# Latent attention rebuilt: three rounded passes for scores and output product, one pipeline over 40 tiles

## The reference

```python
def blocked_attention(q_nope, q_rope, k_nope, k_rope, v):
    scale = 1.0 / math.sqrt(MLA_NOPE + MLA_ROPE)
...
        s = jnp.einsum('bqhd,bkhd->bhqk', qn, k_nope) + jnp.einsum('bqhd,bkd->bhqk', qr, k_rope)
        p = jax.nn.softmax(s.astype(jnp.float32) * scale, axis=-1).astype(v.dtype)
        return jnp.einsum('bhqk,bkhe->bqhe', p, v)
...
def mla_latent(h, ckv_ctx, krope_ctx, cos, sin, w_in, q_norm, kv_norm, w_q_b, w_kv_b, w_out):
...
    k_nope = jnp.concatenate([k_nope_c, k_nope_l], axis=1)
    k_rope_all = jnp.concatenate([krope_ctx, k_rope], axis=1)
    o = blocked_attention(q_nope, q_rope, k_nope, k_rope_all, v)
    return o.reshape(b, n, MLA_HEADS * MLA_V) @ w_out
```

## Time and profile before

| what | us |
|---|---|
| median of 3 runs | 2439.28 (2438.9 to 2439.61) |
| profiled execution | 2436.64 |
| its span | 2434.8 |
| retention, router, mixture of layer 0 (to) | 1352 |
| latent attention: front (from 1352 to) | 1485.76 |
| heads (to) | 1691.89 |
| output product (to) | 1763.26 |
| router and mixture of layer 1 (to) | 2434.8 |

### The profile page before, as it was taken

How to read it: one execution, slowest core, us unless ns; L and a number is a source line. 1 busy time by engine, 2 the same in 40 slices (tenths; PEclk the granted TensorE clock), 3 DMA queues, 4 the chain that set the end, 5 groups by cost and what they waited for, 6 DMA issues and landing times.

```text
span 2434.8 us, 26516 instructions
## 1 busy us (share of the span) xinstructions
PE 2268.7 (93%) x9712; PEld 1502.3 (62%) x9712; DVE 1715.2 (70%) x1882; ACT 1256.0 (52%) x1314; POOL 192.7 (8%) x227
## 2 busy tenths in 40 slices
PE   6999999999986999999999888988959999999995
PEld 2867868768654666666666454554436666666663
DVE  2675665757757899998998441332368998999996
ACT  3321312213135877778776333332347778777773
POOL 1000000000031011001000200000020001110001
PEclk9999999999998999999999899999979999999998
DMA  7443434525355999999998110100069999999991
GB/s 264 126 134 105 138 121 148 163 98 162 102 201 191 360 349 344 360 364 349 354 339 307 45 72 1 36 1 0 1 233 343 357 361 354 357 346 345 339 361 61
DMA packets 167649, 529.10 MB, mean 217 GB/s; under 512 B 13525, under 2 KB 22282, under 8 KB 167306
## 3 DMA queue, kind: packets, MB, share of 16 engines
q1 hardware_dynamic: 162954, 515.35, 59.1%
q0 software_dynamic: 2304, 8.39, 1.0%
q10 hardware_dynamic: 2304, 4.20, 0.5%
HBM read 516.72 MB, written 11.17 MB: 217 GB/s over the span
## 4 chain that ended last, share of the span: by engine, by line
PE 90%; DVE 4%; ACT 3%; issue 1%; POOL 1%; DMA 0%; SPq 0%; POOLq 0%; ACTq 0%; DVEq 0%
PE ps L1606 86%; PE ps L1609 4%; POOL SMALL L578 0%; POOL SMALL L577 0%; ACT W L308 0%; ACT W_HI L308 0%; DVE IDX L1363 0%; DVE B L1189 0%; DVE X L1190 0%; DMA REGION<-in_ada_b_dram 0%; DVE MIXREG L1362 0%; DVE REGION L1581 0%; DVE B L1164 0%; DVE ROUTE L1365 0%; ACT B L722 0%
## 5 line engine op out<-in xcount | busy, mean ns | idle before, releaser
L1401 DVE TENSOR_TENSOR W_LO<-RAW_W,W_HI 128x2048 fp32r<-128x2048 f32 x384 | 867.8, 2287 | 80.2 <-ACT W_HI L308 76.6
L308 ACT ACTIVATE W_HI<-RAW_W 128x2048 fp32r<-128x2048 f32 x384 | 726.4, 1917 | 197.8 <-PE ps L1606 196.8
L1606 PE MATMUL ps<-W_HI,XET_HI 128*80 128x512 f32 x1024 | 323.6, 397 | 17.4 <-issue 11.4
L1606 PE MATMUL ps<-W_LO,XET_HI 128*80 128x512 f32 x1024 | 320.9, 395 | 0.0
L1606 PE MATMUL ps<-W_HI,XET_LO 128*80 128x512 f32 x1024 | 320.8, 395 | 0.0
L1606 PEld LDWEIGHTS ps<-W_HI,XET_HI 128*80 128x80 f32 x1024 | 151.7, 149 | 98.4 <-issue 13.6
L1606 PEld LDWEIGHTS ps<-W_LO,XET_HI 128*80 128x80 f32 x1024 | 152.5, 149 | 86.3 <-issue 1.9
L1606 PEld LDWEIGHTS ps<-W_HI,XET_LO 128*80 128x80 f32 x1024 | 152.5, 149 | 85.2 <-issue 2.1
L1133 DVE SCALAR_TENSOR_TENSOR ADA_SUM<-ADA_RAW,NCOL,ADA_SUM 128x512 f32<-128x512 f32 x280 | 191.1, 744 | 0.0
L1606 PE MATMUL ps<-W_HI,HTE_HI 128*80 128x512 f32 x512 | 166.9, 407 | 8.6 <-issue 8.6
L1606 PE MATMUL ps<-W_LO,HTE_HI 128*80 128x512 f32 x512 | 161.2, 396 | 0.0
(11 more groups left out here) (244 smaller groups left out, 3340.0 us busy)
## 6 DMA issues: line engine op xcount, KB each, us to landing
RAW_W<-in_moe_w_gate_dram SPq DMA_DIRECT2D x128, 1024.0 KB, 5.7
RAW_W<-in_moe_w_up_dram SPq DMA_DIRECT2D x128, 1024.0 KB, 6.1
RAW_W<-in_moe_w_down_dram SPq DMA_DIRECT2D x128, 1024.0 KB, 5.6
ADA_RAW<-in_ada_w_dram SPq DMA_DIRECT2D x80, 512.0 KB, 3.6
RING_RAW<-in_ret_w_in_dram SPq DMA_DIRECT2D x48, 512.0 KB, 4.6
W<-in_ada_w_dram SPq DMA_DIRECT2D x4, 2048.0 KB, 14.2
RING_RAW<-in_ret_w_out_dram SPq DMA_DIRECT2D x16, 512.0 KB, 4.7
xn_rows<-B SPq DMA_DIRECT2D x8, 512.0 KB, 13.4
```

The costliest lines, as they stand in the source:

```text
L308: return nc.scalar.activation(out, in_, ACT.Copy, scale=scale)
L1401: V_.tensor_tensor(W_LO[:, slot], RAW_W[:, slot], W_HI[:, (place + i) % HSLOTS].bitcast(F32), ALU.subtract).then_inc(MS_["lo"], 1)
L1606: return T.matmul(out, lhsT, rhs, start=first, stop=last)
```

## The change

**Scores.** A tile's scores become five fp32r products in splits of 384 and 256 columns: QN_HI by KN_HI, QN_HI by KN_LO, QN_LO by KN_HI, and QS (rotary queries, hi in the upper half of the partitions, lo in the lower) by the two planes of KS. The prompt tile is scored against 256 keys, of which the last 128 are used. DVE makes the low parts out of PSUM (`projected_lo`), and the wait for them replaces that for ACT's copies.

**One pipeline.** The 40 tiles alternate between two pairs of banks, so that a tile waits only for the tile two before it, across heads. The next head's first scores go before the last transposes of a head, and `head_out` is done in two halves of 256 tokens around the first transposes. On DVE the scaling of tile t stands before the maxima of tile t+1.

**Output product.** 240 fp32r products in place of 80 plain ones (of two passes each). The weights are split in eight pieces during the last three heads (`WO_SPLITS`), each by ACT and then DVE, and the heads' outputs are split tile by tile (`heads_hi`, `heads_lo`).

**Fillers and the rest.** `keep_busy` issues plain products of 512 columns whose result is not used: 6 after the first normalisation, 6 and 11 before the lists of the two routers, 4 before the first turn of each mixture, 5 in the latent layer after its gates. The rotary transposes move into the projection of rotary queries and the first values. One of the two memsets of the rotary keys goes. The mirror product stands before the row mask. Some semaphores are merged, and the weights' pieces are loaded at other times (after the projections of heads 3 and 7).

```diff
+        WO_SPLITS = {(5, 3): (0, 2), (5, 4): (0, 3), (6, 3): (0, 0), (6, 4): (0, 1), (7, 1): (1, 0), (7, 2): (1, 1), (7, 3): (1, 2), (7, 4): (1, 3)}
...
                 sp.wait_ge(MA["kn_mm"], MH)
-                sp.dma_start(W4[:, 2], wo[1]).then_inc(w_in[2], 16)
+                sp.dma_start(W4[:, 2], wo[0]).then_inc(w_in[2], 16)
+                sp.wait_ge(MA["kn_mm"], 2 * MH - 1)
+                sp.dma_start(W4[:, 0], wo[1]).then_inc(w_in[0], 16)
...
-                chain.link(nc.gpsimd.memset(KRT[ROPE:P, 0, :], 0.0))
-                chain.link(nc.gpsimd.memset(KRT[0:ROPE, 1, :], 0.0))
+                chain.link(nc.gpsimd.memset(KS[ROPE:P, 1, :].bitcast(F32), 0.0))
...
                     act.wait_ge(MA["kn_mm"], 2 * h + n + 1)
-                    dst = (KNT, QNT)[n][:, h % 2, :]
-                    act_copy(dst, ps[:, 2:4, :].rearrange("p a n -> p (a n)")[:, 0:(NK * P, TOK)[n]]).then_inc(MA["kn_ev"], 1)
+                    dst = (KN_HI, QN_HI)[n][:, h % 2, :]
+                    act_copy(dst, ps[:, 2:4, :].rearrange("p a n -> p (a n)")[:, 0:(NK * P, TOK)[n]]).then_inc(MA["kn_hi"], 1)
...
+                def split_out(h, t):
+                    if (h, t) in WO_SPLITS:
+                        g, k = WO_SPLITS[h, t]
+                        if h > 5:
+                            act.wait_ge(MA["kn_mm"], 2 * MH)
+                        act.wait_ge(w_in[(2, 0)[g]], 16 * BEFORE_MLA[(2, 0)[g]] + (32, 48)[g])
+                        act_copy(WO_HI[g][:, k, :], WO_RAW[g][:, k, :]).then_inc(MA["wo_hi"], 1)
...
+                exps(0, 0)
                 for h in range(MH):
-                    exps(h, 0)
                     for t in range(NT):
-                        if t + 1 < NT:
+                        if t < 3:
                             exps(h, t + 1)
                         if t in (1, 2) and h + 1 < MH:
                             projected(h + 1, t - 1)
-                        act.wait_ge(MA["pt_tr"], NT * h + t + 1)
-                        if t < NLAT:
-                            src = ps[:, 0:2, :].rearrange("p a n -> p (a n)")[:, 0:LAT + P].rearrange("p (k q) -> p k q", q=P)
-                            act_copy(PT[:, :, t * P:(t + 1) * P], src).then_inc(MA["pt_ev"], 1)
-                        else:
-                            act_copy(PTP, ps[:, 0, 0:P]).then_inc(MA["pt_ev"], 1)
+                        weights_across(h, t)
+                        if t == 3:
+                            exps(h, t + 1)
+                        if t == 4 and h + 1 < MH:
+                            exps(h + 1, 0)
+                        split_out(h, t)
...
+                def projected_lo(h, n):
+                    dve.wait_ge(MA["kn_hi"], 2 * h + n + 1)
+                    to = slice(0, (NK * P, TOK)[n])
+                    rest((KN_LO, QN_LO)[n][:, h % 2, :], ps[:, 2:4, :].rearrange("p a n -> p (a n)")[:, to], (KN_HI, QN_HI)[n][:, h % 2, :]).then_inc(MA["kn_ev"], 1)
+
+                def split_out(h, t):
+                    if (h, t) in WO_SPLITS:
+                        g, k = WO_SPLITS[h, t]
+                        dve.wait_ge(MA["wo_hi"], list(WO_SPLITS).index((h, t)) + 1)
+                        rest(WO_LO[g][:, k, :], WO_RAW[g][:, k, :], WO_HI[g][:, k, :]).then_inc(MA["wo_lo"], 1)
...
+                def weights_scaled(h, t):
+
+                    n = NT * h + t
+                    width = LAT + P if t < NLAT else P
+                    dve.wait_ge(MA["e_done"], n + 1)
+                    chain.link(V_.reciprocal(RRC[:, n % 2:n % 2 + 1], RSM[:, n % 2:n % 2 + 1]))
+                    V_.tensor_scalar(PR[:, n % 2, 0:width], PR[:, n % 2, 0:width], RRC[:, n % 2:n % 2 + 1], None, ALU.mult).then_inc(MA["pr"], 1)
...
+                scores_max(0, 0)
                 for h in range(MH):
-                    scores_max(h, 0)
                     for t in range(NT):
+                        weights_scaled(h, t)
+                        if t == 1 and h:
+                            head_out(h - 1, 1)
+                        if t in (2, 3) and h + 1 < MH:
+                            projected_lo(h + 1, t - 2)
                         if t + 1 < NT:
                             scores_max(h, t + 1)
-                        n = NT * h + t
-                        width = LAT + P if t < NLAT else P
-                        dve.wait_ge(MA["e_done"], n + 1)
-                        chain.link(V_.reciprocal(RRC[:, n % 2:n % 2 + 1], RSM[:, n % 2:n % 2 + 1]))
-                        V_.tensor_scalar(PR[:, n % 2, 0:width], PR[:, n % 2, 0:width], RRC[:, n % 2:n % 2 + 1], None, ALU.mult).then_inc(MA["pr"], 1)
+                        elif h + 1 < MH:
+                            scores_max(h + 1, 0)
                         if t == 0 and h:
-                            head_out(h - 1)
-                head_out(MH - 1)
+                            head_out(h - 1, 0)
+                        split_out(h, t)
...
+            def keep_busy(bank, products):
+
+                for _ in range(products):
+                    mm(ps[:, bank, :], IDENT[:], STEP1[:], True, True)
...
+            keep_busy(0, 6)
...
+                keep_busy(0, (6, 11)[layer])
...
-                mm(ps[:, 2, 0:NE * CAPP], ONES[0:NE, :], PM[0:NE].rearrange("p e r -> p (e r)"), True, True).then_inc(MS_["pick_tr"], 1)
-                pe.wait_ge(MS_["pick"], b["pick"] + 3)
                 pe.wait_ge(MS_["zero"], b["zero"] + 1)
                 for w in range(2):
                     last = mm(ps[0:CAP, 1, w * NE:(w + 1) * NE], MIRROR[0:CAP], LISTS[0:CAP, w, 64:ROWS], True, True)
                 last.then_inc(MS_["pick_tr"], 1)
+                pe.wait_ge(MS_["pick"], b["pick"] + 3)
+                mm(ps[:, 2, 0:NE * CAPP], ONES[0:NE, :], PM[0:NE].rearrange("p e r -> p (e r)"), True, True).then_inc(MS_["pick_tr"], 1)
...
+                keep_busy(3, 4)
...
+                keep_busy(7, 5)
...
                     n = NT * h + t
-                    if t >= 2:
+                    if n >= 2:
                         pe.wait_ge(MA["e_done"], n - 1)
-                    elif h:
-                        pe.wait_ge(MA["e_done"], NT * h)
-                    b = (4, 6, 4, 6, 4)[t]
-                    for lo, hi in (((0, HALF), (HALF, LAT + P)) if t < NLAT else ((LAT + P, NK * P),)):
-                        mm(ps[:, b, 0:hi - lo], QNT[:, h % 2, t * P:(t + 1) * P], KNT[:, h % 2, lo:hi], True, False)
-                        last = mm(ps[:, b, 0:hi - lo], QRT[:, h // 2, t * P:(t + 1) * P], KRT[:, h % 2, lo:hi], False, True)
+                    b = 4 + 2 * (n % 2)
+                    q = slice(t * P, (t + 1) * P)
+                    for lo, hi, at in (((0, 3 * P, P), (3 * P, NT * P, 0)) if t < NLAT else ((NLAT * P, NK * P, 0),)):
+                        out, keys = ps[:, b, at:at + hi - lo], slice(lo, hi)
+                        mm(out, QN_HI[:, h % 2, q], KN_HI[:, h % 2, keys], True, False)
+                        mm(out, QN_HI[:, h % 2, q], KN_LO[:, h % 2, keys], False, False)
+                        mm(out, QN_LO[:, h % 2, q], KN_HI[:, h % 2, keys], False, False)
+                        mm(out, QS[h][:, q], KS[:, 0, keys], False, False)
+                        last = mm(out, QS[h][:, q], KS[:, 1, keys], False, True)
                         b += 1
                     last.then_inc(MA["s_mm"], 1)
                 def project_keys(h):
                     for n, (lo, hi) in enumerate(((0, HALF), (HALF, NK * P))):
...
+                        pe.wait_ge(MA["pt_ev"], NT * (h + 1) - 1)
+                    at = slice(part * LAT // 2, (part + 1) * LAT // 2)
                     for kt in range(NT):
-                        last = mm(ps[:, 2, :], B1[:, kt, h * P:(h + 1) * P], PT[:, kt, :], kt == 0, kt == NT - 1)
+                        last = mm(ps[:, 2 + part, 0:LAT // 2], B1[:, kt, h * P:(h + 1) * P], PT[:, kt, at], kt == 0, kt == NT - 1)
+                    if part:
+                        pe.wait_ge(MA["pt_ev"], NT * (h + 1))
+                        last = mm(ps[:, 3, LAT // 2:LAT // 2 + P], VP[:, h * P:(h + 1) * P], PTP, True, True)
                     last.then_inc(MA["o_mm"], 1)
-                    mm(ps[:, 3, 0:P], VP[:, h * P:(h + 1) * P], PTP, True, True).then_inc(MA["o_mm"], 1)
-
-
...
+                scores(0, 0)
                 for h in range(MH):
...
-                pe.wait_ge(w_in[2], base[2] + 32)
-                pe.wait_ge(MA["o_ev"], 2 * MH)
+                    scores(h, 1)
+                    if h:
+                        head_out(h - 1, 0)
+                    weights_across(h, 0)
+                    if h:
+                        head_out(h - 1, 1)
+                    scores(h, 2)
+                    if h + 1 < MH:
+                        project_keys(h + 1)
+                    weights_across(h, 1)
+                    scores(h, 3)
+                    if h + 1 < MH:
+                        project_queries(h + 1)
+                    weights_across(h, 2)
+                    scores(h, 4)
```

(15 more changed lines are left out.)

267 lines of the change are left out of this document (171 added, 96 removed).

## The result

The changed kernel took 2403.75 us (median of 4 runs, 2398.12 to 2404.74) where the kernel before took 2439.12 (4 runs): a ratio of 0.9851, interval 0.9840 to 0.9863, 35 us or 1.5% faster. 2401 had been forecast, in a range of 2385 to 2418. The profiled execution took 2398.12, its span 2396.3, which is 38.5 less than before; the sum made against a profiled execution was -38.1. The profiled execution is the fastest of the four: the other three lie 5 to 7 us above it, at granted clocks of 0.972 to 0.974 for 0.975, and the medians differ by 35.4.

The account below looks back on a forecast made before the run. PE, busy 93% of 2434.8 us, was taken as the bound. Terms of -16.1, -14.0, -0.9, +2.0, -2.0, -0.8 and -6.3 sum to -38.1: 2398.5 from the profiled 2436.64, 2401 on the runs' scale, range 2385 to 2418.

Parts of the forecast that it names:

- Scores and waits of a head: Latent attention: rounded scores and shorter PE waits save 3.94 us a head, 31.5 over eight.
- the narrow product at the fp32 pace: Rival: fp32r score products of 256 columns take 0.427 us instead of 0.120, +61 us, 2462; chance 0.05.
- loads in series: Rival: each score product stands behind its own load of 0.19 us, +64 us, 2465; chance 0.03.
- The splits: Splitting output weights in the last three heads makes PE wait through the queues of ACT and DVE, +13.5 us.
- a fall of the clock behind head 7's waits: Two waits of 4 to 6 us in head 7 may let the clock fall, +2.0 us.
- The output product: Behind attention, 160 passes of 0.43 us become 240 of 0.227, -14.0 us.
- Lead: Before head 0 nothing hides the low parts of keys and queries, +1.9 us.
- rotary transposes: Front of the latent layer: spread into projection and values, they lose the waits between them, -2.0 us.
- Fillers: Idle products before stretches where PE starts at half clock give back 6.3 us, 1.4 of it at the start.
- The splits did not hide: Rival, denied here: ACT and DVE idle enough to hide the splits, 13.5 us less, 2388; chance 0.12.
- the fillers did not overrun: Rival, denied here: fillers at half clock last past their gaps, 9.2 us lost and 6.3 not gained, 2417; chance 0.16.
- the time stay even: Rival: ACT bounds the loop of heads, so PE's waits grow by what scores save, 2436; chance 0.04.

Follow-up runs that it names:

- out_plain: The changed kernel with the output product in plain fp32, without splits of the output weights and heads' outputs: 2398.32 us, ratio 0.9833 to the kernel before.
- splits_later: The changed kernel with DVE's half of each output-weight split one turn behind ACT's half: 2392.55 us, ratio 0.9805 to the kernel before.
- later_heads: As splits_later, with DVE's low part of the first tile's heads moved behind the scaling of head 7's last tile: 2386.76 us, ratio 0.9786 to the kernel before.
- scores_plain: The changed kernel with scores by two plain fp32 products in place of five rounded ones: 2417.15 us, ratio 0.9910 to the kernel before.
- no_fillers: The changed kernel without any of the fillers: 2409.52 us, ratio 0.9880 to the kernel before.
- router_back: The changed kernel with the router's order of before, row mask ahead of the mirror product: 2401.58 us, ratio 0.9844 to the kernel before.

## Why the prediction was right, step by step

**Scores and waits of a head: right.** The paces of 0.120 and 0.173 for 256 and 384 columns, estimated from the line through 320 and 512 columns, are 0.12 and 0.17. Neither the narrow product at the fp32 pace nor loads in series came: with load records of 0.19, products of 256 columns start 0.12 apart. That is against the rule of the Trainium skill's page that was weighed ("TensorE: Matmul & The Clock Gate", Part 3, Packing small matmuls). The head was forecast at 20.4 and took 20.22. The forecast set two waits of 0.56 and 0.50 against 1.42 and 1.09, which are waits of PEld; there they became 0.51 and 0.39. On PE's own rows the 1.23 and 0.89 of the kernel before became 0.34 and 0.18:

```profile
1538.18 0.76 PE L1609 MATMUL ps<-IDENT,REGION 128*128 128x128 f32 x5 [1.23 <-DVE REGION L1581]
...
1539.83 0.30 PE L1609 MATMUL ps<-IDENT,REGION 128*128 128x128 f32 x1 [0.89 <-ACT W L308]
```

Either way a head waits 1.6 less, for the 1.39 of the working. One reason can be read: ACT's two copies start 0.60 apart (1605.88 and 1606.48 in head 5), where the working put their 0.70 end to end.

**The splits: right in mechanism, a little short in size.** 13.5, and 2.0 for a fall of the clock behind head 7's waits, were forecast, less 0.9 for the wait ahead of the output product: 14.6. The 16.5 measured against out_plain, which has that wait (0.74), compare with this. Heads 5 and 6 cost 3.0 and 3.6 for 3.5 each; head 7 cost 9.9 (27.95 us from its first transposes to the output product, for 18.03 in out_plain) for 7.6. The last two waits of head 7 were 4.94 and 3.74:

```profile
1656.71 1.33 PE L1728 MATMUL ps<-IDENT,REGION 128*128 128x128 f32 x5 [4.94 <-DVE REGION L1678]
1661.79 0.47 PE L1728 MATMUL ps<-IDENT,REGION 128*128 128x128 f32 x1 [3.74 <-DVE REGION L1678]
1662.05 0.63 PE L1725 MATMUL ps<-W,B 128*128 128x256 f32 x1
```

The clock fell there as forecast, but not at the start of the output product, which ran at 1.00: it is head 7's own output, 20 products that took 6.13 us at 0.70 (1.8 lost, since they take 4.32 in out_plain). Splits_later and later_heads show what the working had only in part: not ACT's 1.05 and DVE's 1.22 count, but the place where one engine waits for the other ahead of the work that PE wants. The subtraction of the first tile's heads was in the same place and was not in the prediction.

**The stage: 2.9 better than forecast.** The sum's terms for the stretch from the first keys to the output product, -16.1, the clock's 2.0 and the vanished wait's -0.9, make -15.0; it was -17.9. Part of it lay in the kernel before. From the transposes of tile 3 to those of the next head's tile 0 it took 10.69 us in head 1 (1538.18 to 1548.87), and 12.37 in head 2 (1562.50 to 1574.87), 1.7 more. In windows of 12.37 us from either start PE is busy 11.48, but starts 42 products at 1.00 of the clock in the first and 34 at 0.86 in the second:

```profile
1538.18:1550.55 12.37, 11.48 (x42) 6.41 (x43) 3.77 (x10) 3.45 (x7) 0.00 (x0) 1.00 0.00 1
1562.50:1574.87 12.37, 11.48 (x34) 6.14 (x35) 2.90 (x9) 2.75 (x6) 0.00 (x0) 0.86 0.44 160
```

The second window holds SP's load of output weights (the share of 0.44). That the load made the clock fall is not shown: two loads of the same size, 1545 to 1553 and 1624 to 1632, came at a clock of 1.00 in the changed kernel.

So one head had stood for eight, and the head picked was one without that fall. Out_plain, which has the new heads without splits, gives the rest:

```profile
1516.61 0.71 PE L1714 MATMUL ps<-IDENT,REGION 128*128 128x128 f32 x5
...
1638.01 0.71 PE L1714 MATMUL ps<-IDENT,REGION 128*128 128x128 f32 x5
```

These are the transposes of tile 0 of heads 1 and 7, six heads of 20.23 apart: 0.15 a head better than forecast, 0.9 in all. From the first scores to the first of them it is 22.46 us, for 30.74 before, and from the second to the output product 18.03 for 19.72. So heads 0 and 7 together gained 10.0, where the forecast had twice 3.94: 2.1 more, since their order is their own. The 1.7, 0.9 and 2.1 gained, less the 1.9 by which the splits cost more than 14.6, make the 2.9 but for 0.1.

**The output product: right in kind, 1.2 too good.** -14.0 was forecast and -12.8 came. The 240 products start 0.233 apart instead of 0.227 as in retention, at a granted clock of 1.00. The reason stays open; no run tried it.

**Lead, rotary transposes, front.** +1.9 forecast, 1.83 measured (8.05 us from the first keys to the first scores before, 9.88 after); -2.0 for the rotary transposes, -1.97 measured; -0.8 for the memset and nothing for the rotary keys' loop, -2.0 measured for both, the five fillers there included, at 0.79 of the clock before and 0.91 after. The hit on the rotary transposes is luck. The kernel before began that stretch at half clock (0.54 in the first 2 us from 1447.15; its first 20 products took 5.0 us, for 4.1 after), so 0.9 of the 1.97 is the clock and 1.1 the move. The waits between the transposes were 0.39 and 0.29; the third, 0.69 ahead of the first keys, is still there as 0.73. And the stretch took 36.64 us in the execution that was profiled and as much in the traces of scores_plain and no_fillers, but 38.1 to 38.5 in the other six, for 38.61 before.

**Fillers: right in sum, by two misses.** -6.3 forecast; no_fillers says 5.8. Of the 1.4 at the start the changed kernel's trace has next to nothing, and splits_later's has it all. In the two layers 4.9 were forecast. From the picks' transposes to those behind the first expert products no_fillers takes 25.32 us in layer 0 and 25.08 in layer 1, the changed kernel 22.28 and 22.39: the fillers give 5.7. But the kernel before took 24.63 and 24.46 there, also without fillers, so the router's new order costs 0.7 and 0.6, where nothing with 1 us to either side was forecast. This agrees with the 0.7 of router_back, and it is the main reason why the table of stages shows only 4.0 for both layers.

**The sum: luck in part.** -38.1 for the -38.5 of the profiled execution is closer than the terms are: the stage was 2.9 better and the front 1.2, the output product 1.2 worse, and the start with the stretches up to the first expert products 2.7 worse. Over the medians the change is 35.4, for which 2401 was 2.75 too low: the kernel before was profiled 2.5 below its median, the changed one 5.6 below.

**What it says of the rivals.** The splits did not hide (heads 5 to 7), the fillers did not overrun (they ended 1.03 us before the places came in layer 1, and 1.97 before in layer 0), and no narrow product was slow. Nor did the time stay even with ACT as the bound of the loop: heads 1 to 4 fell to 20.2.
